# A two-layer hybrid model step on one core: prompt columns and sample tokens through the weight slabs together, or apart

## The chip, the cores and the metric

The kernel runs on one NeuronCore of a Trainium2 chip. It is one launch; the metric is its device time in microseconds. The core's engines have queues of their own: TensorE (PE, with its weight loads PEld), VectorE (DVE), ScalarE (ACT), GpSimd (POOL) and SyncE (SP, which here issues DMAs). They meet through semaphores.

## The reference, cut to what matters

512 prompt tokens and 8 x 4 = 32 sample tokens, all float32, go through the same weights. Layer 0 has a gated short convolution and an attention with forget gates over a paged cache, layer 1 a Conformer convolution module, and both a feed-forward part with a convolution on its gate branch.

```python
h = rmsnorm(x, norm_g) @ w_in                      # layer 0: 3072 columns and 8 forget gates
yp = yp + jnp.concatenate([ya, yb], axis=-1) @ w_out0[i]
a, g = jnp.split(rmsnorm(x, norm_g) @ w_pw1 + b_pw1, 2, axis=-1)     # layer 1
y, new_hist = causal_dwconv(a * jax.nn.sigmoid(g), hist, conv_w)     # width 31
return jax.nn.silu(layernorm(y + conv_b, ln_g, ln_b)) @ w_pw2, new_hist
gate, val = jnp.split(rmsnorm(x, norm_g) @ w_up, 2, axis=-1)         # both layers, 2816 each
return (jax.nn.silu(causal_dwconv(gate, hist, conv_w)[0]) * val) @ w_down
```

## The kernel before, in words

Activations lie with channels on partitions and T = 544 tokens along: columns 0 to 511 are the prompt (TP = 512), 512 to 543 the samples (TS = 32). A **slab** is one 128-column block of a weight matrix, with 8 tiles of 128x128 (6 or 5 in the down-projections, whose contraction of 2816 is cut in halves of 12 and 10 tiles; there two slabs add into one PSUM group, `per_group` = 2). Slabs go round four slots: SP loads slab s into `w_raw` (`load`), ScalarE copies it to `w_h` in the reduced-precision form fp32r (`split_high`), GpSimd subtracts for the remainder `w_l` (`split_low`). Activations are split the same way into high and low (`xa_h`, `xa_l`; `h_h`, `h_l`). TensorE's `slab` (L1768) makes three products for each tile, `w_h` with high, `w_h` with low and `w_l` with high; since a PSUM bank holds 512 numbers a partition, each runs as two matmuls of HT = 272 columns into the two banks of `pair[0]` or `pair[1]`, in turn.

`plan()` lists the phases: qkv (12 slabs), gates (12), out (8), then for each layer's feed-forward up0 (24 slabs), down0 (16, of 6 tiles), up1 (20), down1 (16, of 5 tiles), and between the two pw1 (16) and pw2 (8). The gates slabs are interleaved with the attention and have a routine of their own (`gate_half`, L2019). Others run through `gemm`, the first turn of four slabs written out, the rest in a loop.

The order on each engine is the order of the code; `turns` walks a phase with four slabs a turn, `ahead` is the preparation of the slab three further on. In an up phase the even slab j is a gate slab, the odd one a value slab. VectorE multiplies the gate slab by 1/rms (`scaled`, L1152), makes the three-tap convolution `cv`; ScalarE `sl` = silu (L1022); GpSimd `sr` = `sl` x 1/rms (L738); VectorE `tmp` = value x `sr` (L1590); ScalarE `h_h` (L1026), VectorE `h_l` (L1592). In `residual` phases VectorE adds the slab to `x` (L1529), and `norm_work` (L800, L801) squares and splits `x` for the next phase. In pw1 VectorE's `chunk` makes `u` and eleven taps of the 31-tap convolution; the others are matmuls in four column groups (`pe_conv`, L2182 and L2185), reading `u_sh`, copies of `u` that SP and ScalarE shift by DMA (`shifted`). In the attention, `value_page` (L1952) multiplies pages of cached values, likewise in four column groups, and `own_heads` (L1959) turns the result. `head_square` and `head_root` (L854, L859, L861) serve the norms of queries and keys in qkv, between slabs of which TensorE sums squares (L1864).

The semaphores that matter: `s_raw` (loaded), `s_hi`, `s_lo` (split), `s_slab` (multiplied), `s_free` or `s_xnew` (read out of PSUM).

## Time and profile before

| | us |
|---|---|
| median of 3 runs | 1512.69 (1512.01 to 1517.98) |
| the profiled execution | 1527.78 |
| its span, first to last instruction | 1525.9 |
| TensorE busy | 1440.1 |
| VectorE, GpSimd, ScalarE busy | 744.6, 587.1, 473.0 |
| mean granted clock of TensorE | 0.971 |

The rows further down are from the profiled execution. TensorE's rows show the start of each matmul and a duration that includes its passage through the array, so that consecutive ones overlap: what one costs in a row of many is the distance between starts, not the duration. An fp32 matmul leaves two records, an fp32r one a single record.

### The profile page before, as it was taken

How to read it: one execution, taken by the hardware profiler on the slowest of the kernel's cores; microseconds unless marked ns; L12 is line 12 of the kernel's file. 1: busy time of each engine (PE TensorE's matmuls, PEld its weight loads, DVE VectorE, ACT ScalarE, POOL GpSimd, SP SyncE). 2: the span in 40 equal slices, each digit the busy share in tenths (PEclk: the TensorE clock that was granted, in tenths of full speed). 3: DMA queues.
4: the chain of work that ended last, by engine and by line, in shares of the span. 5: the costliest groups of instructions: out<-in, count | busy, mean ns of one | idle time of the engine just before them, and what ended most of it. 6: DMA issues, size and time to landing. Idle time of an engine off the chain costs nothing. (4 is left out here: it accounts for less than half of the span.)

```text
span 1525.9 us, 34946 instructions
## 1 busy us (share of the span) xinstructions
PE 1440.1 (94%) x13997; PEld 1326.6 (87%) x13997; DVE 744.6 (49%) x1258; ACT 473.0 (31%) x678; POOL 587.1 (38%) x321
## 2 busy tenths in 40 slices
PE   6998898899799999999999999986999999999998
PEld 5896666666689999999999987864999999999998
DVE  5654766677443544203443369988345441044411
ACT  5374222222134222312223331116443322222221
POOL 3312222222232645445444344430435444445441
PEclk9999988999989999999999999997999999999999
DMA  5416777987732332233322446560313323323222
GB/s 177 125 52 217 244 250 256 316 281 232 237 100 69 100 93 69 84 97 96 89 70 61 131 124 158 145 159 15 109 56 92 93 70 94 107 79 91 62 78 73
DMA packets 246375, 192.56 MB, mean 126 GB/s; under 512 B 12129, under 2 KB 205106, under 8 KB 246186
## 3 DMA queue, kind: packets, MB, share of 16 engines
q1 hardware_dynamic: 244753, 188.71, 40.6%
q10 hardware_dynamic: 1373, 1.84, 0.5%
q8 instruction: 77, 1.26, 0.3%
q0 software_dynamic: 144, 0.52, 0.1%
q14 instruction: 28, 0.23, 0.0%
HBM read 173.03 MB, written 6.04 MB: 117 GB/s over the span
## 5 line engine op out<-in xcount | busy, mean ns | idle before, releaser
L664 POOL TENSOR_TENSOR w_l<-w_raw,w_h 128x1024 fp32r<-128x1024 f32 (+2 forms) x195 | 432.9, 2222 | 447.6 <-ACT w_h L791 418.8
L1768 PE MATMUL banks<-xa_h,w_h 128*128 128x272 f32 x1856 | 388.2, 290 | 4.5 <-DVE tmp L1590 3.3
L1768 PE MATMUL banks<-xa_h,w_l 128*128 128x272 f32 x1856 | 384.9, 289 | 0.0
L1768 PE MATMUL banks<-xa_l,w_h 128*128 128x272 f32 x1856 | 383.6, 288 | 0.0
L1768 PEld LDWEIGHTS banks<-xa_h,w_h 128*128 128x128 f32 x1856 | 293.3, 189 | 6.8 <-issue 5.5
L1768 PEld LDWEIGHTS banks<-xa_l,w_h 128*128 128x128 f32 x1856 | 292.6, 189 | 0.0
L1768 PEld LDWEIGHTS banks<-xa_h,w_l 128*128 128x128 f32 x1856 | 290.5, 189 | 0.0
L791 ACT ACTIVATE w_h<-w_raw 128x1024 fp32r<-128x1024 f32 (+2 forms) x193 | 185.1, 961 | 182.5 <-PE banks L1768 182.2
L1768 PE MATMUL banks<-h_h,w_h 128*128 128x272 f32 x960 | 202.4, 292 | 8.1 <-DVE h_l L1737 8.0
L1768 PE MATMUL banks<-h_h,w_l 128*128 128x272 f32 x960 | 200.7, 291 | 0.0
L1768 PE MATMUL banks<-h_l,w_h 128*128 128x272 f32 x960 | 200.2, 290 | 0.0
L1529 DVE TENSOR_TENSOR x<-banks,x 128x544 f32 (+1 forms) x48 | 34.8, 725 | 271.5 <-PE banks L1768 271.5
L1768 PEld LDWEIGHTS banks<-h_h,w_h 128*128 128x128 f32 x960 | 153.2, 191 | 10.0 <-issue 7.5
L1768 PEld LDWEIGHTS banks<-h_l,w_h 128*128 128x128 f32 x960 | 153.2, 191 | 0.0
L1768 PEld LDWEIGHTS banks<-h_h,w_l 128*128 128x128 f32 x960 | 152.0, 191 | 0.0
L738 POOL TENSOR_TENSOR sr<-sl,r_all 128x544 f32<-128x544 f32 x44 | 59.8, 1360 | 232.8 <-ACT sl L1022 232.8
L1022 ACT ACTIVATE sl<-cv 128x544 f32<-128x544 f32 x44 | 29.0, 659 | 276.8 <-DVE cv L1585 276.7
L685 POOL TENSOR_SCALAR sb<-sb,small 128x128 f32<-128x128 f32 (+3 forms) x32 | 34.7, 1083 | 180.0 <-DVE small L1336 180.0
L1152 DVE TENSOR_TENSOR gate<-banks,r_all 128x544 f32<-128x544 f32 x44 | 31.8, 724 | 110.5 <-PE banks L1768 104.7
L1590 DVE TENSOR_TENSOR tmp<-banks,sr 128x544 f32<-128x544 f32 x44 | 31.9, 725 | 107.5 <-POOL sr L738 107.5
L1262 DVE STREAM_TRANSPOSE k_grp<-k_grp 128x2048 f32<-128x2048 f32 x32 | 73.5, 2298 | 0.4 <-DMA k_grp<-in_cache_k 0.4
L1576 DVE SCALAR_TENSOR_TENSOR cv<-gate,params,cv 128x511 f32<-128x511 f32 x88 | 66.1, 751 | 12.7
(286 smaller groups left out, 1698.4 us busy)
## 6 DMA issues: line engine op xcount, KB each, us to landing
w_raw<-in_w_up SPq DMA_DIRECT2D x88, 512.0 KB, 3.6
k_grp<-in_cache_k SPq DMA_DIRECT2D x128, 256.0 KB, 4.1
v_pg<-in_cache_v SPq DMA_DIRECT2D x128, 256.0 KB, 5.2
w_raw<-in_w_in SPq DMA_DIRECT2D x24, 512.0 KB, 6.5
w_raw<-in_w_down SPq DMA_DIRECT2D x32, 384.0 KB, 3.1
w_raw<-in_w_pw SPq DMA_DIRECT2D x24, 512.0 KB, 4.1
w_raw<-in_w_down SPq DMA_DIRECT2D x32, 320.0 KB, 3.1
w_raw<-in_w_out SPq DMA_DIRECT2D x8, 512.0 KB, 6.3
```

The source lines that it names most:

```text
L664: g.tensor_tensor(w_l[:, slot, 0:n], w_raw[:, slot, 0:n], w_h[:, slot, 0:n].bitcast(F32), ALU.subtract).then_inc(s_lo, 1)
L685: g.tensor_scalar(sb[:, k % 2, 0:n], sb[:, k % 2, 0:n], rinv[:, w:w + 1], None, ALU.mult).then_inc(s_pn, 1)
L738: g.tensor_tensor(sr[:, j // 2, :], sl[:, j // 2, :], r_all[:, :], ALU.mult)\
L791: A(w_h[:, slot, 0:n], w_raw[:, slot, 0:n], ACT.Copy).then_inc(s_hi, 1)
L1022: A(sl[:, b, :], cv[:, b, :], ACT.Silu).then_inc(s_sl, 1)
L1152: V.tensor_tensor(halves(dst), gview(b), halves(r_all[:, :]), ALU.mult).then_inc(s_free, 1)
L1262: V.transpose(k_grp[slot][:, at, :].rearrange("p g x -> p (g x)"), k_grp[slot][:, at, :].rearrange("p g x -> p (g x)")).then_inc(s_tk, 1)
L1529: V.tensor_tensor(halves(flat(x[:, ds(m, 1), :])), gview(q % 2), halves(flat(x[:, ds(m, 1), :])), ALU.add).then_inc(s_xnew, 1)
L1576: V.scalar_tensor_tensor(yp, gate[:, b, 0:TP - n], w, yp, ALU.mult, ALU.add)\
L1590: V.tensor_tensor(halves(tmp[:, b, :]), gview(1), halves(sr[:, b, :]), ALU.mult).then_inc(s_free, 1)
L1768: ins = mm(out[:, half, 0:HT], w, v[:, half * HT:(half + 1) * HT], start=first and t == 0 and n == 0, stop=last and t == phase.tiles - 1 a ...
```

## The change

- The prompt's 512 columns go through each slab as one matmul per product, into one bank (`wide_bank[q][:, 0:TP]`). VectorE reads a pair's 544 columns in one piece (`gview`).
- The 32 sample tokens are computed apart (`sample_part`): for each tile, the sample activations in full fp32 (`xs_in`, `xa_s` or `h_s`, 128x32) are stationary and the raw weights `w_raw` (128x128) are moving. Tile t goes to column group t mod 4, so four partial sums of 32 tokens x 128 channels stand on the four quarters of the partitions (`by_token`, in the pair's second bank). ScalarE copies them to SBUF (`tokens_read`, into `tok_q` or `tok_f`), and one more fp32 matmul with `four_q` or `four_f` (four stacked 32x32 identities) adds the four and turns them to channels on partitions (`sample_turned`, into columns 512 to 543).
- `sample_part` stands in the middle of a slab, `sample_turned` before the last tile of a bank group. In the first bank group of a phase the part comes behind the slab, and the turn within the next slab.
- `w_raw` is read by TensorE too, so SP's next load of a slot waits for the sample part (`s_part`) instead of for GpSimd (`s_lo`).
- ScalarE copies the sample columns of activations separately in fp32 (`xa_s`, `h_s`), and high and low parts cover 512 columns. In up phases silu moves from the even to the odd turn.
- In pw1 SP issues `shifted` before the loads, two slabs earlier in the code.
- The constants, memory places, and the changed calls in qkv, pw1, pw2 and the mixers follow the same pattern and are left out here.

```diff
+    def part(self, i, j):
+
+        return i * 4 + (self.parts0 + j)
+
+    def sums(self, i, j):
+
+        return i * (4 // self.per_group) + (self.sums0 + j // self.per_group)
...
-        gview = lambda b: pair[b][:, :, 0:HT]
+        hview = lambda b: pair[b][:, :, 0:HT]
+        wide_bank = [pair[b].rearrange("p k c -> p (k c)") for b in range(2)]
+        gview = lambda b: wide_bank[b][:, 0:T]
+        by_token = lambda b: wide_bank[b][:, TP + P:TP + 2 * P]
+        tok_of = lambda phase: tok_q if phase.name == "qkv" else tok_f
...
             def load(phase, i, j, src):
                 s = phase.slab(i, j)
                 if not (isinstance(s, int) and s < SLOTS):
-                    sp.wait_ge(s_lo, s - (SLOTS - 1))
+                    sp.wait_ge(s_part, phase.part(i, j) - (SLOTS - 1))
                 sp.dma_start(w_raw[:, j, 0:phase.tiles * P].rearrange("p (k n) -> p k n", n=P), src)\
...
             for s in range(24):
                 i, j = s // 4 % 4, s % 4
+                if 6 <= s < 22 and s % 2 == 0:
+                    shifted(s // 2 - 3)
                 if s < 16:
                     load(ph["pw1"], i, j, cols(a["w_pw1"][0], i * (2 * P) + ((j % 2) * D + (j // 2) * P)))
                 else:
                     load(ph["pw2"], i, j, cols(a["w_pw2"][0], i * 512 + j * P))
-                if s >= 8 and s % 2 == 0:
-                    shifted(s // 2 - 4)
...
                 apart(m)
                 A(sq[:, b, :], x[:, ds(m, 1), :].rearrange("p a t -> p (a t)"), ACT.Square).then_inc(s_sq, 1)
-                A(xa_h[:, ds(m, 1), :].rearrange("p a t -> p (a t)"), x[:, ds(m, 1), :].rearrange("p a t -> p (a t)"),
+                A(xa_s[:, ds(m, 1), TP:T].rearrange("p a t -> p (a t)"),
+                  x[:, ds(m, 1), TP:T].rearrange("p a t -> p (a t)"), ACT.Copy, scale=par(name, m + g0)).then_inc(s_xs, 1)
+                A(xa_h[:, ds(m, 1), 0:TP].rearrange("p a t -> p (a t)"), x[:, ds(m, 1), 0:TP].rearrange("p a t -> p (a t)"),
                   ACT.Copy, scale=par(name, m + g0)).then_inc(s_xhi, 1)
+
...
+            def tokens_read(phase, i, j):
+
+                q, n = (j // phase.per_group) % 2, phase.sums(i, j)
+                act.wait_ge(s_part, phase.part(i, j) + 1)
+                if not (isinstance(n, int) and n < 2):
+                    act.wait_ge(s_turn, n - 1)
+                A(tok_of(phase)[:, q, :], by_token(q), ACT.Copy).then_inc(s_tok, 1)
...
                             b = j // 2
-                            if j % 2 == 0:
+                            tokens_read(pu, i, j)
+                            if j % 2:
                                 act.wait_ge(s_cv, k + 1)
                                 if not (isinstance(k, int) and k < 2):
                                     act.wait_ge(s_sr, k - 1)
                                 A(sl[:, b, :], cv[:, b, :], ACT.Silu).then_inc(s_sl, 1)
-                            else:
                                 act.wait_ge(s_free, pu.group(i, j) + 1)
                                 apart(i)
-                                A(h_h[:, ds(i * 2 + b, 1), :].rearrange("p a t -> p (a t)"), tmp[:, b, :],
+                                A(h_s[:, ds(i * 2 + b, 1), TP:T].rearrange("p a t -> p (a t)"), tmp[:, b, TP:T],
+                                  ACT.Copy).then_inc(s_xs, 1)
+                                A(h_h[:, ds(i * 2 + b, 1), 0:TP].rearrange("p a t -> p (a t)"), tmp[:, b, 0:TP],
                                   ACT.Copy).then_inc(s_hhi, 1)
                     turns(act, pu, turn, peel=1 if l == 0 and half == 0 else 0)
...
+            def slab_done(phase, i, j):
+
+                dve.wait_ge(s_slab, phase.slab(i, j) + 1)
+                dve.wait_ge(s_turn, phase.sums(i, j) + 1)
+
+            def scaled(dst, phase, i, j, b):
+
+                slab_done(phase, i, j)
+                V.tensor_tensor(dst, gview(b), r_all[:, :], ALU.mult).then_inc(s_free, 1)
...
-                        dve.wait_ge(s_slab, phase.slab(i, (q + 1) * phase.per_group - 1) + 1)
-                        V.tensor_tensor(halves(flat(x[:, ds(m, 1), :])), gview(q % 2), halves(flat(x[:, ds(m, 1), :])),
-                                        ALU.add).then_inc(s_xnew, 1)
+                        slab_done(phase, i, (q + 1) * phase.per_group - 1)
+                        V.tensor_tensor(flat(x[:, ds(m, 1), :]), gview(q % 2), flat(x[:, ds(m, 1), :]), ALU.add)\
+                         .then_inc(s_xnew, 1)
...
+            def sample_part(phase, i, j, moving):
+
+                q, first, last = (j // phase.per_group) % 2, j % phase.per_group == 0, j % phase.per_group == phase.per_group - 1
+                for t in range(phase.tiles):
+                    k, at = t + (0 if first else phase.tiles), 32 * (t % 4)
+                    xs = xs_in[:, k, :] if phase.name == "qkv" else moving(k)[2]
+                    ins = mm(by_token(q)[at:at + 32, :], xs, w_raw[:, j, t * P:(t + 1) * P],
+                             start=first and t < 4, stop=last and t >= phase.tiles - 4)
+                ins.then_inc(s_part, 1)
+
+            def sample_turned(phase, i, j):
+
+                q = (j // phase.per_group) % 2
+                pe.wait_ge(s_tok, phase.sums(i, j) + 1)
+                mm(wide_bank[q][:, TP:T], tok_of(phase)[:, q, :], (four_q if phase.name == "qkv" else four_f)[:, :],
+                   start=True, stop=True).then_inc(s_turn, 1)
...
-                out = pair[(j // phase.per_group) % 2]
+                out = wide_bank[(j // phase.per_group) % 2][:, 0:TP]
+                late = isinstance(i, int) and i == 0 and j < phase.per_group
                 for t in range(phase.tiles):
                     k = t + (0 if first else phase.tiles)
                     if ready:
                         ready(k)
-                    hi, lo = moving(k)
+                    if t == 2 and isinstance(i, int) and i == 0 and j == phase.per_group and phase.name != "qkv":
+                        sample_turned(phase, 0, 0)
+                    if t == phase.tiles // 2 and not late:
+                        sample_part(phase, i, j, moving)
+                    if t == phase.tiles - 1 and last and not late:
+                        if phase.name == "qkv" and i == 0 and j == 1:
+                            sample_turned(phase, 0, 0)
+                        sample_turned(phase, i, j)
+                    hi, lo, _ = moving(k)
                     wh, wl = w_h[:, j, t * P:(t + 1) * P], w_l[:, j, t * P:(t + 1) * P]
                     for n, (w, v) in enumerate(((wh, hi), (wh, lo), (wl, hi))):
-                        for half in range(2):
-                            ins = mm(out[:, half, 0:HT], w, v[:, half * HT:(half + 1) * HT],
-                                     start=first and t == 0 and n == 0,
-                                     stop=last and t == phase.tiles - 1 and n == 2)
+                        ins = mm(out, w, v[:, 0:TP], start=first and t == 0 and n == 0,
+                                 stop=last and t == phase.tiles - 1 and n == 2)
                 ins.then_inc(s_slab, 1)
+                if late:
+                    if phase.name == "qkv":
+                        pe.wait_ge(s_xs, 1)
+                    elif phase.name == "out":
+                        pe.wait_ge(s_four, 3)
+                    sample_part(phase, i, j, moving)
```

TensorE in the loop of an up phase, from the end of one slab into the next; in before each row of x2 is the two halves of 272 columns:

```order
L1768 MATMUL banks<-xa_h,w_h 128x272 x2
L1768 MATMUL banks<-xa_l,w_h 128x272 x2
L1768 MATMUL banks<-xa_h,w_l 128x272 x2
L1768 MATMUL banks<-xa_h,w_h 128x272 [waits free,lo]
L1768 MATMUL banks<-xa_h,w_h 128x272
L1768 MATMUL banks<-xa_l,w_h 128x272 x2
```

The same place now, from the middle of the slab to the next one:

```order
L1857 MATMUL banks<-xa_h,w_l 128x512
L1822 MATMUL banks<-w_raw,xa_s 32x128 x8
...
L1829 REGISTER_ALU
L1830 MATMUL banks<-four_f,tok_f 128x32 [waits sample_copied]
L1857 MATMUL banks<-xa_h,w_h 128x512
L1857 MATMUL banks<-xa_l,w_h 128x512
L1857 MATMUL banks<-xa_h,w_l 128x512
L1837 REGISTER_ALU
L1874 REGISTER_ALU [waits lo]
L1857 MATMUL banks<-xa_h,w_h 128x512 [waits free]
```

Two rows of 272 columns have become one of 512, and two blocks of another kind stand among them, the second with a wait for ScalarE.

ScalarE in the same loop before, one turn's first half (even and odd slab of the first pair):

```order
L791 ACTIVATE w_h<-w_raw 128x1024 [waits slab]
L1019 ISA
L1021 REGISTER_ALU [waits conv]
L1022 ACTIVATE sl<-cv 128x544 [waits silu_r]
L788 ISA
L790 ISA [waits raw0]
L791 ACTIVATE w_h<-w_raw 128x1024 [waits slab]
L1024 ISA
L1026 ISA [waits constants,free]
L1026 ACTIVATE h_h<-tmp 128x544
```

and now, from the odd slab's part of the turn:

```order
L821 ACTIVATE w_h<-w_raw 128x1024 [waits slab]
L839 REGISTER_ALU
L841 REGISTER_ALU [waits sample_part]
L842 ACTIVATE tok_f<-banks 128x128 [waits sample_turned]
L1068 ISA
L1070 REGISTER_ALU [waits conv]
L1071 ACTIVATE sl<-cv 128x544 [waits silu_r]
L1072 REGISTER_ALU
L1074 ISA [waits constants,free]
L1074 ACTIVATE h_s<-tmp 128x32
L1076 ISA
L1076 ACTIVATE h_h<-tmp 128x512
```

The copy of the partial sums stands between the split of the next weights and silu, and silu behind both splits.

SP in pw1 before:

```order
L414 DMA w_raw<-in_w_pw 128x8x128 [waits lo] x9
L591 DMA u_sh_140<-u 32x784 [waits conv_cleared,u]
L591 DMA u_sh_140<-u 32x784 x3
L591 DMA u_sh_140<-u 32x783 x4
L414 DMA w_raw<-in_w_pw 128x8x128 [waits lo] x2
```

and now:

```order
L441 DMA w_raw<-in_w_pw 128x8x128 [waits sample_part] x6
L621 DMA u_sh_147<-u 32x784 [waits conv_cleared,u]
L621 DMA u_sh_147<-u 32x784 x3
L621 DMA u_sh_147<-u 32x783 x4
L441 DMA w_raw<-in_w_pw 128x8x128 [waits sample_part] x2
```

Six loads instead of nine stand ahead of the first shifted copies, and the loads wait for TensorE's sample part.

## Rows read from the trace of the kernel before

**Rows 1.** The page: span, TensorE's busy time, its 40 slices, the granted clock.
```profile
span 1525.9 us, 34946 instructions
PE 1440.1 (94%) x13997; PEld 1326.6 (87%) x13997; DVE 744.6 (49%) x1258; ACT 473.0 (31%) x678; POOL 587.1 (38%) x321
PE   6998898899799999999999999986999999999998
PEclk9999988999989999999999999997999999999999
```
**Rows 2.** Busy time by stage; columns in the first row, x is the count.
```profile
core 0: us, PE busy (x) PEld busy (x) DVE busy (x) ACT busy (x) POOL busy (x), PEclk, DMA share, GB/s
500.00:600.00 100.00, 100.00 (x800) 100.00 (x800) 48.83 (x97) 27.39 (x35) 53.82 (x27) 1.00 0.30 90
136.00:138.00 2.00, 2.00 (x17) 2.00 (x16) 0.18 (x1) 0.00 (x0) 0.00 (x0) 1.00 1.06 406
332.00:341.00 9.00, 8.73 (x229) 6.33 (x227) 7.31 (x17) 3.11 (x4) 2.93 (x2) 1.00 0.79 277
389.00:393.00 4.00, 4.00 (x59) 3.64 (x58) 0.42 (x1) 0.62 (x2) 2.38 (x1) 1.00 0.06 19
...
908.00:1036.00 128.00, 114.20 (x1336) 88.82 (x1339) 115.16 (x141) 25.39 (x42) 50.63 (x21) 0.96 0.58 149
```
**Rows 3.** TensorE's waits: total us, times, longest.
```profile
PE banks L2182 <- DMA u_sh<-u: 9.6, 7, 3.6
PE banks L1768 <- DVE h_l L1737: 8.0, 4, 7.1
```
**Rows 4.** TensorE in time, up stage: start, duration, line, shapes, count.
```profile
546.80 0.41 PE L1768 MATMUL banks<-xa_h,w_h 128*128 128x272 f32 x2
...
548.81 0.41 PE L1768 MATMUL banks<-xa_h,w_l 128*128 128x272 f32 x2
```
**Rows 5.** TensorE in time: 256-column matmuls into value pages.
```profile
389.91 0.28 PE L2019 MATMUL banks<-xa_h,w_l 128*128 128x256 f32 x1
...
390.99 0.28 PE L2019 MATMUL banks<-xa_h,w_l 128*128 128x256 f32 x1
391.20 1.06 PE L1952 MATMUL banks<-v_pg,pr 128*8 128x128 f32 x32
```
**Rows 6.** TensorE in time: 288-column matmuls, then 64-row ones.
```profile
136.28 0.29 PE L2019 MATMUL banks<-xa_h,w_h 128*128 128x288 f32 x1
...
138.55 0.29 PE L2019 MATMUL banks<-xa_h,w_l 128*128 128x288 f32 x1
138.77 0.48 PE L1969 MATMUL banks<-qkv 64*128 64x256 f32 x1
```
**Rows 7.** TensorE in time: the convolution's matmuls, 32 stationary columns.
```profile
911.16 1.06 PE L2182 MATMUL banks<-u_sh,w_sh 128*32 128x512 f32 x8 [2.67 <-DMA u_sh<-u]
912.01 0.24 PE L2185 MATMUL banks<-u_sh,w_sh 128*32 128x32 f32 x5
```
**Rows 8.** TensorE in time: value pages, then a full-width transpose.
```profile
339.92 1.06 PE L1952 MATMUL banks<-v_pg,pr 128*8 128x128 f32 x32
340.91 0.33 PE L1979 MATMUL banks<-ident,sb 128*128 128x128 f32 x1
```
**Rows 9.** TensorE in time: own_heads and its neighbour.
```profile
336.25 0.40 PE L1959 MATMUL banks<-small,own 128*128 128x16 f32 x2
336.49 0.27 PE L1924 MATMUL banks<-ident,small 128*32 128x128 f32 x1
```
**Rows 10.** Line 918: ScalarE's copies out of PSUM, ns shortest/median/longest.
```profile
L918 ACT ACTIVATE pt<-banks x32: 255/426/581, 146.3 to 389.0; 128x128 f32<-128x128 f32 x8, 128x256 f32<-128x256 f32 x8, 128x384 f32<-128x384 f32 x8, 128x512 f32<-128x512 f32 x8
```
**Rows 11.** ScalarE and VectorE in time, up stage.
```profile
560.91 0.66 ACT L1022 ACTIVATE sl<-cv 128x544 f32<-128x544 f32 x1 [7.46 <-DVE cv L1585]
563.99 0.66 ACT L1026 ACTIVATE h_h<-tmp 128x544 f32 x1 [1.47 <-DVE tmp L1590]
564.56 1.04 ACT L791 ACTIVATE w_h<-w_raw 128x1024 fp32r<-128x1024 f32 x1
568.80 0.72 DVE L1152 TENSOR_TENSOR gate<-banks,r_all 128x544 f32<-128x544 f32 x1 [2.74 <-PE banks L1768]
```
**Rows 12.** TensorE and ScalarE in time, qkv stage.
```profile
75.21 1.08 PE L1864 MATMUL banks<-sq,head_ones 128*128 128x272 f32 x4
80.57 0.64 ACT L854 ACTIVATE sq<-qkv 128x544 f32<-128x544 f32 x1
81.23 1.28 ACT L859 ACT_TABLE_LOAD   x1
```
**Rows 13.** The page, DMA issues: count, size, us from issue to landing.
```profile
w_raw<-in_w_up SPq DMA_DIRECT2D x88, 512.0 KB, 3.6
w_raw<-in_w_down SPq DMA_DIRECT2D x32, 320.0 KB, 3.1
```

More of the change, by code:

```diff
@@ L106, in plan @@
         slab, groups[residual] = p.slab1, p.group1
+    part = sums = 0
+    for p in phases.values():
+        if p.name != "gates":
+            p.parts0, p.sums0 = part, sums
+            part, sums = part + p.slabs, sums + p.slabs // p.per_group
     return phases
@@ L197, in build @@
         base = top[0]
+        xa_s, _ = place("xa_s", [P, DC, T], F32, xa_at)
+        h_s, _ = place("h_s", [P, HALF[0], T], F32, hh_at)
         x_rows, _ = place("x_rows", [P, 5, D], F32, hh_at)
@@ L847, in _ @@
             A(fw_h[:, :, :], fw[:, :, :], ACT.Copy).then_inc(s_fw, 1)
+            for n in range(2):
+                tokens_read(ph["qkv"], 0, n)
             root(0)
@@ L876, in _ @@
                     head_square(n - 3)
+                if n >= 2:
+                    tokens_read(ph["qkv"], n // 4, n % 4)
                 if n == 4:
@@ L989, in _ @@
             act.wait_ge(s_sp, NGRP)
+            A(h_s[:, 4:8, TP:T], qkv[:, 0:4, TP:T], ACT.Copy).then_inc(s_xs, 1)
             for c in range(4):
-                A(h_h[:, 4 + c, :], qkv[:, c, :], ACT.Copy).then_inc(s_hhi, 1)
+                A(h_h[:, 4 + c, 0:TP], qkv[:, c, 0:TP], ACT.Copy).then_inc(s_hhi, 1)
             def residual(phase, stage, then=None, late=None):
@@ L1513, in _ @@
                 dve.wait_ge(s_hhi, 5 + c)
-                V.tensor_tensor(h_l[:, 4 + c, :], qkv[:, c, :], h_h[:, 4 + c, :].bitcast(F32), ALU.subtract)\
+                V.tensor_tensor(h_l[:, 4 + c, 0:TP], qkv[:, c, 0:TP], h_h[:, 4 + c, 0:TP].bitcast(F32), ALU.subtract)\
                  .then_inc(s_hlo, 1)
```

73 lines of the change are left out of this document (47 added, 26 removed).

## The prediction

> **What bounds the kernel now.** I read the page first, then windows by stage, then waits, then TensorE's own rows in time. TensorE is busy 1440.1 of 1525.9 us at a granted clock of 9 tenths or more in nearly every slice [rows 1]. In an up stage (500 to 600 us) it is busy without a gap, at full clock, while VectorE has 48.83, ScalarE 27.39 and GpSimd 53.82 of the 100 us [rows 2]. What it waits for there is about nothing; over the kernel the largest waits in the slabs are 9.6 us for u_sh transfers and 8.0 us for h_l [rows 3]. So outside the Conformer's first projection (pw1), whatever TensorE gains or loses in a slab is gained or lost in the end. In pw1 (908 to 1036 us) VectorE has 115.16 of 128 us and TensorE idles 13.8 [rows 2]: there VectorE sets the pace.
>
> **The old slab.** 16 matmuls of 272 columns start between 546.80 and 548.81 us, so one starts every 125.5 ns [rows 4] (800 in 100 us less the two that straddle the edge gives 125.3 [rows 2]; I use 125.3). A tile of the weights takes six, 752 ns. The work: 132 slabs of 8 tiles (qkv 12, out 8, up 88, pw1 16, pw2 8), 32 of 6 and 32 of 5 in the down phases, in all 1408 tiles, 8448 matmuls. The `gates` slabs aren't touched.
>
> **Term 1, wide prompt matmuls.** Each pair of 272 columns (250.6 ns) becomes one of 512. No fp32r matmul of 512 columns stands in the trace. Two other widths do: 256 columns start every 120 ns (389.91 to 390.99, nine steps) and 288 every 133 (136.28 to 138.55, seventeen steps) [rows 5, 6]. At 2.4 GHz, the level of full granted clock in these stretches, the columns alone are 106.7, 113.3 (for 272) and 120.0 ns, so there is an excess of 12 to 13.5 ns. If the excess is fixed per matmul, 512 columns take 213.3 + 12.7 = 226 ns; if it grows with the columns (0.461 ns each), 236. I take 230, between them. Below that end I go to the excess of the fp32 streams, which is small: two rounds of 512 fp32 columns at two cycles each take 0.85 us where the columns are 853 ns [rows 7]; then 215.8 (a rival below). At 230 a matmul saves 20.6 ns: 494 ns in a slab of 8 tiles, 742 in two slabs of 6, 618 in two of 5.
>
> **Term 2, the sample part.** A slab gets one fp32 matmul per tile: stationary 128x32 sample activations, moving 128 raw weight columns, in four column groups. The trace has nearly the same thing: the value pages (L1952), stationary 128x8, moving 128x128 fp32, four column groups. Each such matmul leaves two records. 32 records start from 339.92, the last is 0.79 us later (1.06 of the row less 0.27 of one), and the next kind starts at 340.91 [rows 8]. So eight rounds of four: seven steps and the 20 ns inside a round make 0.79, a round is 110 ns, which is the 128 columns at two cycles. Eight tiles are 16 records, four rounds: 3 x 110 + 20 = 0.35 us to the last start, plus 0.20 to the next full-width matmul. On the way in, the full-width matmul before it is followed after 0.21 instead of 0.12 (390.99 to 391.20) [rows 5], and 0.22 instead of 0.13 into a row-split kind (138.55 to 138.77) [rows 6]: +0.09. In all 0.35 + 0.20 + 0.09 = **0.64 us** a slab. Six and five tiles need the same four rounds, since tiles 4 and 5 reuse groups 0 and 1. Thirty-two stationary columns instead of eight should not matter: the convolution's matmuls have 32 and eight records of 512 columns, in two rounds, take 0.85 us [rows 7]. The lower bound is the rounds alone, 0.44.
>
> Nothing of this lies beside other TensorE work. It replaces 96 columns per tile (three passes of 32, 40 ns) by two records of 128 columns at two cycles, a quarter each, 55 ns: **the stream doesn't get shorter**, only the excess of three matmuls per tile does.
>
> **Term 3, adding and turning.** One fp32 matmul, stationary tok 128x128, moving 128x32, once per bank group: 132 + 32 = 164. Nearest is own_heads (L1959), stationary 128x128, moving 16: its two records start at 336.25, the next kind at 336.49 [rows 9], so 0.245 us, set by the weight loads, as 32 moving columns are 27 ns. Bounds: 0.055 (streams alone) and 0.245 plus a wait for ScalarE. I take **0.245**. The first bank group of each phase does its sample part behind its slab and turns within the next; the prices are the same.
>
> **What the other engines do.** ScalarE copies the 128x128 partial sums first; 128 columns out of PSUM took 255 ns [rows 10], and the turn stands before the last tile, three tiles (2.1 us) after the sample part in a slab of 8, two tiles (1.4 us) in one of 6 or 5. Queued behind the copy's wait on ScalarE are the split of the next weights, silu and h_h. In the up stage a gate slab ends at about 568.4, where VectorE's `gate` product is released (568.80), so the slabs before it end at 562.4 and 556.4; silu begins at 560.91, 4.5 us into the odd slab, h_h ends at 564.65, 2.2 us into the even one, and the next split at 565.6, 3.2 into it [rows 11]; the new copy is due at 0.64 + 4 x 0.69 = 3.4 and must be over by 5.5: covered. In qkv the cycle is tight: the head sums begin at 75.21 and take four records of 0.23, so the next slab begins at 76.1; ScalarE's square ends at 81.21 and the table load follows [rows 12]; the copy goes between them, to 81.5, against the turn at 76.1 + 5.5 = 81.6. I book 1 us for the eight slabs. A w_raw slot now comes free at the middle of its slab's matmuls instead of when GpSimd is done. SP's load then lands 3.1 us (down) or 3.6 us (up) later [rows 13], about 1.2 us into the next slab, and is first read by ScalarE's split just then, three slabs before TensorE needs it: nothing, though with 5 tiles (4.1 us a slab) the split and the copy end 2.3 us into the slab against the turn at 3.4, so 1.1 us of cover is left. The h_s and xa_s copies (0.2 us) sit in the same slack; where h_l is awaited (8.0 us [rows 3]) VectorE's chain sets it. In pw1 slabs 6.2 us longer in all hide in the 13.8 us of idleness; SP is moved to issue u_sh's transfers before the loads, and its loads' new waits (middle of slabs already run) hold up nothing.
>
> **The sum.** Slab of 8: -494 + 640 + 245 = +391 ns, times 116 = +45.4 us. Pair of 6: -742 + 1280 + 245 = +783, times 16 = +12.5. Pair of 5: -618 + 1525 = +907, times 16 = +14.5. With 1 us of qkv: **+73 us**. The profiled span goes from 1525.9 to about 1599; that execution took 1527.78 where the median is 1512.69, so the forecast is 1512.7 + 73 = **1586 us**. With 226 ns it is 1570, with 236 ns 1608.
>
> **Rivals.**
> - Wide matmuls nearly free of excess (215.8 ns). For: fp32 streams show 2 ns. Against: three fp32r widths all show 12 to 13.5. Then +50, +272 and +481 ns: +18 with qkv's 1 us, 1531 us. Chance 0.14. The Trainium skill, page "TensorE: Matmul & The Clock Gate", section "Back-to-back issue gap", gives N/2.4 + 2.5 ns for a warm matmul, which would make this the case; the fp32r rows disagree with it.
> - Faster: the array hides the changes of tiling and the turn's weight loads beneath running matmuls. Then the sample part costs 0.43, the turn 0.055, and with 226 ns a slab of 8 gains 107 ns: 1503; with 215.8 also, 1464. It decides where sample part and turn together fall under 0.59 us in a slab of 8. Against: 0.20 and 0.09 stand at every such change I read. 0.06; and 0.04 for a partial case within 0.5%. The skill's page "TensorEngine Tiling (Array Packing)", "When to Use Tiling", advises just this swap for 32 moving columns, with fourfold column tiling; its section "Key Properties" says that changing the mode drains the engine, and the 0.09 and 0.20 are that.
> - The turn waits for ScalarE, whose order puts splits or norms first. Half of 148 turns at 0.5 us: +37, 1623. For: only 0.1 and 1.1 us of cover in qkv and the 5-tile slabs. 0.08.
> - The granted clock drops because more of the time is drains: 0.9 over the 800 us of up and down stages is +80, 1666. Against: value pages and convolution ran at full clock. 0.04.
> - The change doesn't do what it says: four groups run one after another, 16 x 110 ns instead of 4 x 110 for 8 tiles: 1.3 us more in 116 slabs, 0.9 in 32 and 0.7 in 32, about +200, 1790. Against: [rows 7, 8]. 0.02.
>
> **How the numbers follow.** The forecast (226 to 236 ns, changes paid) has 0.62. The range takes in its 1570 to 1608, the first rival's 1531 and the third's 1623, and leaves out the rest, 0.16: 1528 to 1625. Faster by over 0.5% 0.06, within 0.5% 0.04, slower 0.90; 0.5% is about what a measurement of this kernel can tell from no change.
>
> **What would show it.** In an up stage: prompt matmuls starting every 226 to 236 ns; 16 sample records in 0.35 us with 0.09 more before and 0.20 after; a turn of 0.245; slabs of 6.4 us instead of 6.01; TensorE waits on tok near nothing except in qkv; pw1 no longer than before. I am wrong if the pitch is near 216 ns, if records of sample part and full-width matmuls overlap without the gap, or if waits behind tok_q or tok_f exceed a few us.

## The result, and the profile after

The changed kernel takes **1638.03 us** (median of 4 runs, 1634.55 to 1638.82) where the kernel before takes 1515.34 beside it (4 runs, 1512.01 to 1518.71): a ratio of 1.0805, 95% interval 1.0771 to 1.084. The forecast was 1586, with a range of 1528 to 1625. The direction was right; of a loss of 123 us it foresaw 73. Of parts_only, further down, one of the four executions took 2377.65 us at a granted clock of 0.558; its median is that of the other three.

The head of the page of after, to be read against [rows 1]; the first line gives span and instructions, then busy time by engine, then the slices of TensorE and its granted clock:

```profile
span 1636.7 us, 33584 instructions
...
PE 1537.9 (94%) x12917; PEld 1141.9 (70%) x12917; DVE 691.2 (42%) x1262; ACT 528.2 (32%) x923; POOL 574.0 (35%) x321
...
PE   6998889997999999999998989977989999999998
PEclk9999999998999999999999999988999999999999
```

TensorE has 1080 matmul records fewer and is busy 98 us longer, at much the same mean granted clock (0.978, before 0.971). One piece of an up stage, TensorE's rows in time (start, duration, line, result and operands, shapes, count), to be read against [rows 4]:

```profile
707.39 0.39 PE L1857 MATMUL banks<-xa_h,w_h 128*128 128x512 f32 x1
707.63 0.39 PE L1857 MATMUL banks<-xa_l,w_h 128*128 128x512 f32 x1
707.86 0.40 PE L1857 MATMUL banks<-xa_h,w_l 128*128 128x512 f32 x1
708.18 0.65 PE L1822 MATMUL banks<-w_raw,xa_s 128*32 128x128 f32 x16
708.76 0.50 PE L1857 MATMUL banks<-xa_h,w_h 128*128 128x512 f32 x1
709.09 0.39 PE L1857 MATMUL banks<-xa_l,w_h 128*128 128x512 f32 x1
709.32 0.39 PE L1857 MATMUL banks<-xa_h,w_l 128*128 128x512 f32 x1
...
710.00 0.40 PE L1857 MATMUL banks<-xa_h,w_l 128*128 128x512 f32 x1
710.24 0.30 PE L1830 MATMUL banks<-four_f,tok_f 128*128 128x32 f32 x2
710.38 0.48 PE L1857 MATMUL banks<-xa_h,w_h 128*128 128x512 f32 x1
710.70 0.39 PE L1857 MATMUL banks<-xa_l,w_h 128*128 128x512 f32 x1
```

Wide matmuls start every 0.23 us (232 ns where nothing else stands between them: wide_only's slabs of 5.573 us, below, over 24). Around the 16 sample records the starts are: last wide matmul to first record 0.32, the records 0.37 to the last start, then 0.20 to the first wide matmul (708.76), **and from that one to the next 0.33 instead of 0.23** (709.09). Around the turn: 0.24, 0.14, and again 0.32 to the second wide matmul (710.70). A slab takes 6.533 us where it took 6.013. What TensorE waits for, over the kernel and then in pw1 alone (us in total, times, longest), against [rows 3]:

```profile
PE banks L1830 <- ACT tok_f L842: 25.1, 10, 4.7
PE banks L1857 <- DVE h_l L1801: 9.2, 6, 7.1
...
PE banks L2259 <- DMA c_row<-in_state_conv_c: 5.4, 1, 5.4
...
PE banks L2277 <- DMA u_sh<-u: 3.4, 1, 3.4
```

```profile
ACT w_h L821 <- DMA w_raw<-in_w_pw: 55.1, 7, 9.6
...
PE banks L1830 <- ACT tok_f L842: 16.6, 7, 3.9
```

**By stage.** The length of a phase is read off the starts of its first and last prompt matmul in the records; "before" is a second profiled execution of the kernel before (span 1513.1 us, run beside the first experiments), "expected" is the prediction's sum laid out by phase.

| stage | before | after | difference | expected |
|---|---|---|---|---|
| qkv | 98.2 | 102.3 | +4.1 | +5.7 |
| gates and attention | 299.6 | 280.5 | -19.1 | 0 |
| out | 50.2 | 53.3 | +3.1 | +3.1 |
| four up phases | 536.0 | 587.8 | +51.8 | +34.4 |
| four down phases | 277.3 | 320.8 | +43.5 | +27.0 |
| pw1 | 132.7 | 163.3 | +30.6 | 0 |
| pw1 to pw2 | 33.4 | 35.6 | +2.2 | 0 |
| pw2 | 53.9 | 59.4 | +5.5 | +3.1 |
| sum | | | +121.8 | +73.3 |

The spans differ by 123.6, so the table holds all but 1.8 us. Three things were missed: the slabs cost more, pw1 grew by 30 us where nothing was expected, and the attention became 19 us shorter.

### The profile page after: what moved, and what is told of

Read it like the earlier page. It is cut to its first block, busy times and chain, and to the rows that moved or that the text cites. A ratio compares the mean times of both kernels' runs of the same rounds, so it can differ in the third digit from the quotient of the medians.

```text
span 1636.7 us, 33584 instructions
## 1 busy us (share of the span) xinstructions
PE 1537.9 (94%) x12917; PEld 1141.9 (70%) x12917; DVE 691.2 (42%) x1262; ACT 528.2 (32%) x923; POOL 574.0 (35%) x321
## 4 chain that ended last, share of the span: by engine, by line
PE 80%; issue 5%; DVE 5%; DMA 4%; ACT 3%; SPq 2%; POOL 1%; ACTq 1%; DVEq 0%; POOLq 0%
PE banks L1857 58%; PE banks L1822 6%; PE banks L2114 4%; SPq L621 2%; PE banks L1993 1%; PE banks L1830 1%; PE banks L2047 1%; DMA w_raw<-in_w_pw 1%; DMA v_pg<-in_cache_v 1%; PE banks L2087 1%; PE banks L2064 1%; DVE k_grp L1325 1%; PE banks L2001 1%; ACTq L1118 1%; POOL w_l L694 1%
## 5 line engine op out<-in xcount | busy, mean ns | idle before, releaser
L1857 PE MATMUL banks<-xa_h,w_h 128*128 128x512 f32 x928 | 391.8, 422 | 0.8 <-POOL w_l L694 0.4
L1857 PE MATMUL banks<-xa_h,w_l 128*128 128x512 f32 x928 | 368.4, 397 | 0.0
L1857 PE MATMUL banks<-xa_l,w_h 128*128 128x512 f32 x928 | 368.1, 397 | 0.0
L1857 PEld LDWEIGHTS banks<-xa_h,w_h 128*128 128x128 f32 x928 | 176.9, 191 | 54.2 <-issue 23.6
L1857 PE MATMUL banks<-h_h,w_h 128*128 128x512 f32 x480 | 204.3, 426 | 9.3 <-DVE h_l L1801 9.2
L1857 PEld LDWEIGHTS banks<-xa_h,w_l 128*128 128x128 f32 x928 | 176.3, 190 | 39.4
L1857 PEld LDWEIGHTS banks<-xa_l,w_h 128*128 128x128 f32 x928 | 177.0, 191 | 30.7
L1857 PE MATMUL banks<-h_l,w_h 128*128 128x512 f32 x480 | 190.7, 397 | 0.0
L1857 PE MATMUL banks<-h_h,w_l 128*128 128x512 f32 x480 | 190.6, 397 | 0.0
L1857 PEld LDWEIGHTS banks<-h_h,w_h 128*128 128x128 f32 x480 | 91.3, 190 | 44.9 <-issue 23.6
```

Source lines behind the costliest of these rows:

```text
L1857: ins = mm(out, w, v[:, 0:TP], start=first and t == 0 and n == 0, stop=last and t == phase.tiles - 1 and n == 2)
```

## The experiments

### The three terms one by one

The question: are the three terms of a slab what the sum has, or does the rest of the loss come from somewhere else? Three kernels take parts of the change away, a fourth is the kernel before itself.

wide_only (no sample matmuls, no turns):

```diff
-                    if t == phase.tiles // 2 and not late:
-                        sample_part(phase, i, j, moving)
...
-                dve.wait_ge(s_turn, phase.sums(i, j) + 1)
+                dve.wait_ge(s_part, phase.part(i, j) + 1)
...
             def sample_turned(phase, i, j):
+                return
```

(A prompt matmul in the middle of the slab signals `s_part`.)

> Leaves out the sample matmuls, ScalarE's copies of the partial sums and the turning matmuls; the sample columns are not computed. The semaphore of the sample part is raised by a prompt matmul at the same place. Both theories below have the same value here: 4224 matmuls of 512 columns every 231 ns (measured in the changed kernel) for 8448 of 272 every 125.3, so -83 us: about 1432 against 1515 of before. If the pitch is not what the up stage shows, or other waits come up, it is off by more than 10 us.

parts_only adds the sample part again, turns_only the copies and turns instead:

> The sample matmuls are there, the copies and the turning matmuls left out, so the sample columns are not computed. Theory A (leaving the column groups costs 0.31 us and not 0.20, since the first full-width matmul afterwards takes 0.1 longer; a part is 0.77): 196 x 0.77 = +151 us over wide_only, about 1583. Theory B (a part costs the 0.64 of the prediction and the excess is waits for ScalarE and SP): +125, about 1557.

> The sample matmuls are left out, the copies of the partial sums and the turning matmuls are there, so the sample columns are wrong. Theory A: 164 turns of 0.22 = 36 us, and the waits for ScalarE's copy at three phase starts (12 us) and in pw1 (some 13 us): +61 over wide_only, about 1493. Theory B: 40 us and more waits, +77 or more.

> The kernel before once more, for its profile: the attention stage from the end of qkv to the first out slab took 306.8 us in the first profile and 280.5 in the changed kernel's. If that difference is chance, this profile has a stage well under 300 and a span near 1512; if the change made it, 306 again.

| kernel | median us | ratio to before (95%) | slab of 8, us |
|---|---|---|---|
| wide_only | 1480.89 | 0.9761 (0.971 to 0.9812) | 5.573 |
| turns_only | 1532.24 | 1.0118 (1.0058 to 1.0177) | 5.773 |
| parts_only | 1599.49 | 1.0546 (1.0475 to 1.0616) | 6.33 |
| changed kernel | 1638.03 | 1.0805 (1.0771 to 1.084) | 6.533 |

Slab by slab the three terms are clean: the wide matmuls gain **0.440 us** (0.494 booked), the turn costs **0.200** (0.245 booked), the sample part **0.757** (0.640 booked). Together +0.52, as in after. In the totals part and turn come to 119 and 51 us over wide_only, where their theories A had 151 and 61. Phase by phase against wide_only, the part's shortfall lies in pw1 (9 us of its 12 don't show), qkv (6), up00 and up10 (3 each) and an attention stage 5.5 us shorter; in down00 and up01 it is paid in full. And the wide matmuls brought only 35 us, not the 83 expected, where the slabs alone gain 132 x 0.44 + 32 x 0.34 + 32 x 0.28 = 78 us. Something took more than half of it; that is the question of the third group of experiments. before_again took 1514.96 us, its attention stage 299.6, where the first profile of the same kernel had 306.8.

### What the sample part consists of

The sample part of slabs of 8 is done twice: in one kernel in direct succession, in the other (the diff) at a quarter and at half of the slab. In the first the tiling is entered and left once, in the second twice.

```diff
+                    if t == phase.tiles // 4 and phase.tiles == DC and not late:
+                        sample_part(phase, i, j, moving, False)
                     if t == phase.tiles // 2 and not late:
                         sample_part(phase, i, j, moving)
```

> The changed kernel with each sample part in the middle of a slab of 8 tiles issued twice in direct succession (124 of them; the second starts its sums anew). Theory A (a part is 0.37 us of rounds plus 0.40 of going in and out of the column groups): four more rounds, 0.39 each, +48 us, some less in pw1: about 1682. Theory B (the prediction's prices, rounds 0.44, changes 0.29): +55, about 1692. The kernel after this one decides between them.

> The same number of sample matmuls as in the kernel before this, but the first set two tiles earlier, so that the column groups are entered and left twice. Theory A: 0.40 us more each than together, so +48 us over it, about 1730. Theory B: 0.29 - 0.09 for what rounds hide, 0.20 to 0.29 each, +25 to +36, at most 1720. If changes of tiling cost nothing, the same as together.

1698.14 us together (ratio 1.1178, 1.1131 to 1.1225), 1737.23 apart (1.1432, 1.1386 to 1.1479). TensorE's rows in time, first of the kernel with both together, then of the other:

```profile
756.34 0.40 PE L1860 MATMUL banks<-xa_h,w_l 128*128 128x512 f32 x1
756.66 1.08 PE L1822 MATMUL banks<-w_raw,xa_s 128*32 128x128 f32 x32
757.68 0.50 PE L1860 MATMUL banks<-xa_h,w_h 128*128 128x512 f32 x1
758.01 0.40 PE L1860 MATMUL banks<-xa_l,w_h 128*128 128x512 f32 x1
```

```profile
765.62 0.65 PE L1822 MATMUL banks<-w_raw,xa_s 128*32 128x128 f32 x16
766.19 0.50 PE L1860 MATMUL banks<-xa_h,w_h 128*128 128x512 f32 x1
766.53 0.39 PE L1860 MATMUL banks<-xa_l,w_h 128*128 128x512 f32 x1
...
767.78 0.64 PE L1822 MATMUL banks<-w_raw,xa_s 128*32 128x128 f32 x16
```

Sixteen more records in succession make the slab 6.973 us, 0.440 more than 6.533: four rounds of 110 ns. Apart it is 7.307, another **0.334 us for one more way in and out**. So 0.44 of a part is streaming and 0.33 is the change of tiling, for which the sum had 0.20 (its 0.64 less four rounds); a single part, 0.757, leaves 0.32. The totals agree in kind: 60 us more together (theory B's price of rounds had 55), another 39 apart, between B's 36 and A's 48. The stream alone, 0.440, already eats the 0.440 that the wide matmuls gain in a slab of 8, and more than they gain in the shorter ones: by these prices this way of treating the samples can't win in the slabs even with the change of tiling and the turn at nothing.

### Where the wide matmuls' gain went, and pw1's 30 us

The suspicion: SP's new order and waits hold up pw1. In wide_only, ScalarE's splits wait 69.0 us for `w_raw` loads in pw1; the 16 `u_sh` transfers stand in SP's queue ahead of every second load. Against it stands the prediction's reading, that VectorE sets pw1's pace. The kernel before with the new order (the diff), and the changed kernel with one load ahead of the transfers:

```diff
                 i, j = s // 4 % 4, s % 4
+                if 6 <= s < 22 and s % 2 == 0:
+                    shifted(s // 2 - 3)
...
-                if s >= 8 and s % 2 == 0:
-                    shifted(s // 2 - 4)
```

> The kernel before with only SP's order in pw1 as the change has it: the shifted copies two slabs earlier, ahead of the loads, which wait for GpSimd as before. Theory S: TensorE does not wait for a turn here, so at most the splits are later; within 5 us of before. Rival (the early copies themselves slow pw1 down, as pw1 is 10 us longer in wide_only although its matmuls are shorter): +10 us or more, 1525.

> The changed kernel, in pw1 with SP's next even load issued ahead of the 16 shifted copies instead of behind them (but for the last). Theory S (in pw1 ScalarE's split waits for a load that stands behind 9.6 us of issues, the copy of the partial sums stands behind that split, and TensorE's turn behind the copy): 13 of the 16.6 us of waits in pw1 go, about 1623. Rival (the waits come from ScalarE's own DMA issues and the square root at the phase's start): at most -3 us, 1635.

The first: 1537.71 us, ratio 1.014 (1.0093 to 1.0187); pw1 146.8 instead of 132.7, the gap behind it 40.8 instead of 33.4. **The order alone costs the kernel before some 20 us**, and the higher of the two expectations was still too low. The second: 1646.99 us (1.0845, 1.0794 to 1.0895), pw1 165.4: both expectations missed. In its pw1 the waits for tok fell from 16.6 to 7.4 us, and waits for `u_sh` of 13.6 came in their place: the wait moved. With two loads ahead, the nearest to the order before:

> Nothing is left out. Against the changed kernel (1638.0 us) only SyncE's order in pw1 changes: two loads, then the 16 u_sh transfers of a block, the closest to the order before that the new load waits allow. Theory (ScalarE's split_high waits for loads that stand behind u_sh transfers): with both loads ahead, w_h's waits for w_raw fall from 55 us to under 25, pw1 falls from 163 to 145 to 152 us and the total to 1620 to 1627. Rival (with one load ahead the wait had only moved to u_sh; with two it moves there again): pw1 160 or more, PE's waits for u_sh 10 us or more, total 1635 to 1650.

1704.9 us (1.1261, 1.1225 to 1.1297), 67 more than the changed kernel, and pw1 takes 210.5. The waits in its pw1:

```profile
PE banks L2279 <- DMA u_sh<-u: 51.9, 6, 10.0
...
ACT w_h L823 <- DMA w_raw<-in_w_pw: 21.5, 6, 3.8
```

The split's waits fell as expected, and the rest went wrong: the load of slab 2c+7 now waits until TensorE has done the sample part in the middle of slab 2c+3, right behind which the convolution needs block c of `u_sh`, whose 16 transfers stand behind that load and take 10 us to issue. No order of one queue serves both: what ties them is that a load waits for TensorE. Two kernels remove that tie. One is wide_only with before's waits and order:

```diff
-                    sp.wait_ge(s_part, phase.part(i, j) - (SLOTS - 1))
+                    sp.wait_ge(s_lo, s - (SLOTS - 1))
```

> Work left out: the sample tokens' products and the turns, so their columns of the output are wrong; all else is computed. Against the wide-matmul kernel (1480.9 us) only SyncE changes: its loads wait for GpSimd's split again (s_lo), and the u_sh transfers stand behind the loads as in the kernel before. The wide slabs themselves gain 0.44 us x 132 slabs (and 0.33 x 32, 0.28 x 32), about 75 us, of which only 35 arrived; pw1 had grown by 10 us and the wait for c_row took 5.5. Theory (SyncE's new order and waits ate part of the gain): pw1 128 to 134 us, no c_row wait, total 1455 to 1468. Rival (VectorE and ScalarE set the pace of pw1, and the order does not matter): within 4 us of 1480.9.

The other keeps all matmuls, but moves the high halves through the sample part, so that nothing but the splits reads `w_raw`, and it has before's waits and order too:

```diff
-                    ins = mm(by_token(q)[at:at + 32, :], xs, w_raw[:, j, t * P:(t + 1) * P],
+                    w = w_h[:, j, t * P:(t + 1) * P].bitcast(F32)
+                    ins = mm(by_token(q)[at:at + 32, :], xs, w,
...
-                    sp.wait_ge(s_part, phase.part(i, j) - (SLOTS - 1))
+                    sp.wait_ge(s_lo, s - (SLOTS - 1))
```

> What is changed in the computation: the sample products take the high halves of the weights (w_h) as moving operand instead of the raw weights, so the samples' outputs are less exact; number, shape and type of all matmuls stay. With that, nobody but the splits reads w_raw, so SyncE's loads wait for GpSimd's split as in the kernel before, and the u_sh transfers stand behind the loads as there. Theory S (TensorE's reading of the raw weights binds SyncE's loads to TensorE, which costs pw1 some 20 us, pw1 to pw2 a few and the c_row wait 5): slabs still 6.533 us, pw1 140 to 146 us instead of 163, no c_row wait, total 1605 to 1612. Rival R (the tok copies behind the splits and the root, and VectorE, set pw1's length whatever SyncE does): pw1 158 or more, total 1628 to 1638.

wide_loads_as_before takes **1454.83 us**, ratio 0.9621 (0.9584 to 0.9657): 26 less than wide_only by nothing but SP's waits and order. pw1 fell from 144.3 to 127.9 us, down01 from 72.0 to 62.5 (c_row's wait of 5.5 is gone), the gap behind pw1 from 43.6 to 32.9. With slabs of 5.573 us as in wide_only, 60 of the 78 us now arrive. Of the other 18, qkv holds the most: its twelve slabs gain 5.3 and it takes 98.4 us, as before; what holds it was not tried. high_half_moving takes 1619.09 us (1.0681, 1.0646 to 1.0716), 19 less than the changed kernel; pw1 is 148.1, the gap 33.2. It is nearer to S than to R, though S had 140 to 146 for pw1 and a total under 1612. Waits and order went back together here, so how the 19 us divide between them is not shown. The waits in its pw1, where the splits no longer wait for a load, and a window over it (us, then busy time of PE, PEld, DVE, ACT, POOL with instructions, the clock, DMA share and GB/s):

```profile
ACT w_h L818 <- PE banks L1855: 19.0, 7, 2.9
...
PE banks L1828 <- ACT tok_f L839: 7.4, 2, 4.2
```

```profile
913.00:1061.00 148.00, 139.78 (x1300) 94.14 (x1299) 82.36 (x144) 34.81 (x61) 57.19 (x24) 0.98 0.52 136
```

What is left of pw1's growth, 148.1 less 132.7, is sixteen slabs at 0.52 (8.3) and the waits for tok (7.4). TensorE is busy 140 of 148 us, and VectorE 82.

### The waits at the starts of phases

ScalarE's first copy of partial sums stands behind `root()`, which waits for VectorE's sums; `c_row`'s load stands behind all of down01's loads, which now wait for TensorE.

```diff
             def ffn(l):
+                tokens_read(ph[f"up{l}0"], 0, 0)
                 root(SQ["out" if l == 0 else "pw2"])
```

(The same ahead of pw1's root; the copy in the turn is left out, and `c_row` is loaded after down01's first turn.)

> Nothing is left out. Against the changed kernel (1638.0 us): at the start of up00, up10 and pw1 ScalarE copies the first partial sums ahead of the root, and SyncE issues the c_row load after the first turn of down01's loads. Theory: the three starts lose 3.3 + 4.7 + about 3.5 us of TensorE's wait on tok_f, and c_row's 5.4 goes: total 1638 - 16 = 1622 (1619 to 1626). Rival (the root was late because VectorE's sums are late, so TensorE waits for the same VectorE chain a little later): total within 5 us of 1638.

> Nothing is left out. Both edits in one: two loads ahead of the u_sh transfers, and the early copy and c_row. If they are independent the gains add: 1638 - 16 - (the gain of the order alone); by the theory 1604 to 1612, by its rival 1622 to 1636. In either case it stays above the kernel before (1515), since the up-stage slabs alone cost 60 us more: this is the bound on what the new waits contribute.

> As the kernel before this one in the call (samples from the high halves of the weights), and in addition ScalarE copies the first partial sums of up00, up10 and pw1 ahead of the root. If both causes are right and apart, the total is that kernel's less 8 us, 1597 to 1604, and what is left over the kernel before is the slabs alone: 116 x 0.52 + 16 x 1.07 + 16 x 1.15 + 16 x 0.52 = 104 us less what pw1 hides. If the waits were one and the same, no gain over the other kernel.

copy_and_c_row_early takes 1626.63 us (1.0749, 1.0712 to 1.0786), 11.4 less, where 16 was expected: down01 is 6.6 us shorter, so c_row's part is as expected, and up00, up10 and pw1 together only 6.5, little more than half of what their waits had shown. The waits moved on by a turn. In up00 3.3 us at the first turn became 2.4 at the next, in up10 4.7 became 2.4, and in pw1 3.2 and 3.9 became one of 6.2, so that the sum over the kernel fell only from 25.1 to 22.2:

```profile
PE banks L1837 <- ACT tok_f L845: 22.2, 10, 6.2
```

The other kernels of this group: all_three, with the order of two_loads_before_shift, takes 1689.47 (1.1149, 1.1108 to 1.119), 15 less than that kernel, with pw1 still at 211.5. high_half_and_copy_early takes 1610.74 (1.0632, 1.0598 to 1.0666), 8.4 less than high_half_moving: the two causes are apart, and 94 us over the kernel before beside it (1516.33) are left.

### Splitting the samples off as a matmul of their own

The kernel before with 512 + 32 columns instead of 272 + 272, all in fp32r, with nothing in column groups:

```diff
-                        for half in range(2):
-                            ins = mm(out[:, half, 0:HT], w, v[:, half * HT:(half + 1) * HT],
+                        for a0, a1 in ((0, TP), (TP, T)):
+                            ins = mm(out[:, a0:a1], w, v[:, a0:a1],
```

> Nothing is left out. The kernel before, but each pair of matmuls of 272 columns is one of 512 prompt columns and one of 32 sample columns (same stationary weights, same fp32r passes), results in one span of 544 columns over two banks. Before, a pair takes 251 ns; the 512 columns alone measured 231. Theory A (the excess over the columns grows with them, 0.46 ns each): 32 columns cost 15 to 27 ns, the pair 246 to 258, total 1500 to 1535. Theory B (each matmul has its own weight load, as many LDWEIGHTS as MATMULs in the profile, and a load of 128 columns does not fit under 32): the pair 285 ns or more, slab 6.85 us or more, total 1635 or more. Under B the sample columns can't simply be split off, and 272 + 272 is the better cut.

**2034.93 us**, ratio 1.3418 (1.3365 to 1.3471), 400 us above the least that theory B had. Two stretches of it, TensorE in an up stage (a row holds the matmul of 512 and that of 32) and in out, then windows over both (out first):

```profile
700.13 0.50 PE L1772 MATMUL banks<-xa_h,w_h 128*128 128x512 f32 x2
700.48 0.49 PE L1772 MATMUL banks<-xa_l,w_h 128*128 128x512 f32 x2
```

```profile
499.61 0.80 PE L1772 MATMUL banks<-h_l,w_h 128*128 128x512 f32 x2
500.25 0.80 PE L1772 MATMUL banks<-h_h,w_l 128*128 128x512 f32 x2
```

```profile
445.00:568.00 123.00, 123.00 (x386) 104.33 (x385) 18.75 (x27) 18.60 (x26) 18.98 (x8) 0.50 0.14 41
610.00:770.00 160.00, 160.00 (x931) 139.32 (x930) 45.95 (x101) 31.03 (x39) 59.68 (x30) 1.00 0.21 61
```

At full clock a pair takes 344 ns (a slab 8.267 us), where 272 + 272 take 251 and 512 alone 231. The 32 columns thus cost 113 ns, though their stream is 13. That is the side of theory B, but double its 55 ns; as each matmul has a weight load of its own, and the load behind the 32 columns is as long as any other (PEld 139 of 160 us; the two loads of a pair start 108 ns apart, at 700.108 and 700.216), the loads fit, but that they are the cause was not tested. All eight slabs of out and of pw2 ran at a granted clock of 0.50 on top (1.2 GHz), 15.36 us each: 113 of the 519 us, the longer pairs being nearly all the rest (93 ns times 4224 is 393).

## Why the prediction was wrong, point by point

- **Wide matmuls: right in kind, 2 ns short.** 232 ns, from ends of 226 and 236 and a choice of 230; over 4224 matmuls the 2 ns are 9 us (0.440 for 0.494 in a slab). The Trainium skill, page "TensorE: Matmul & The Clock Gate", section "Back-to-back issue gap", gives N/2.4 + 2.5 ns for an isolated warm matmul, an estimate of 215.8 for 512 columns, and about 131 ns for 512 columns in a sustained stream. The trace agrees with neither: at 256, 272, 288 and 512 columns it has 13.3, 12, 13.5 and 19 ns over the columns. The excess grows somewhat with the columns, less than in proportion.
- **The sample part: right in its mechanism, too small in one term.** The rounds of 110 ns, the 0.09 in and the 0.20 out were all there. The step that failed is "plus 0.20 to the next full-width matmul": I stopped counting at the *start* of the first matmul behind the change, and that one then holds its successor up by another 0.10 us (708.76 to 709.09). 0.757 in place of 0.640. The Trainium skill, page "TensorEngine Tiling (Array Packing)", section "Key Properties", says that a change of mode drains the engine; the runs fit that and give the price, 0.334 us in and out.
- **The turn**: 0.200 for 0.245.
- A slab of 8 came to +0.52 in place of +0.391, a pair of 6 to 80.5 less 72.0 over eight pairs, +1.06 (booked 0.783), a pair of 5 to 75.7 less 66.5 over eight, +1.15 (booked 0.907). In all about +95 us of slabs where 73 were booked: 22 of the 50 missed.
- **"In pw1 slabs 6.2 us longer in all hide in the 13.8 us of idleness"**: wrong, and with it the first part, that VectorE sets the pace there. The window that I read, 908 to 1036 us [rows 2], is not pw1, whose slabs run from 883.4 to 1017.5. Cut at 1017, it has 5.9 us of TensorE's idleness inside pw1 and 7.9 in the 19 us behind it. In the second execution of the same kernel TensorE is busy 129 of 132 us of pw1, and VectorE 90 where the first had 115 of 133. The windows, two of the first execution and one of the second:

```profile
908.00:1017.00 109.00, 103.13 (x1200) 84.17 (x1200) 99.69 (x117) 21.11 (x34) 49.88 (x21) 1.00 0.59 149
1017.00:1036.00 19.00, 11.08 (x138) 4.65 (x141) 15.47 (x25) 4.28 (x8) 0.74 (x1) 0.73 0.54 149
```

```profile
876.00:1008.00 132.00, 128.88 (x1392) 108.94 (x1391) 89.68 (x144) 30.22 (x44) 61.01 (x25) 0.99 0.59 152
```

  The same taps took 1.06 us each in the first execution and 0.72 in others (the two lines below, of before and of high_half_moving), and pw1 was no more than 1.4 us longer for it. A stage that does not follow a change of 25 us in an engine's work isn't bound by that engine. TensorE was the bound, with a few us of waits: wide_loads_as_before shortened pw1 by 4.8 us (its slabs alone by 7.0), high_half_moving lengthened it by 15.4 (its slabs alone by 8.3, and the waits for tok by 7.4).

```profile
L1670 DVE SCALAR_TENSOR_TENSOR tmp<-u,params,tmp 128x488 f32<-128x488 f32 (+4 forms) x34 | 36.1, 1062 | 0.0
```

```profile
L1731 DVE SCALAR_TENSOR_TENSOR tmp<-u,params,tmp 128x490 f32<-128x490 f32 (+4 forms) x35 | 25.0, 716 | 0.0
```

- **"Its loads' new waits (middle of slabs already run) hold up nothing"**: wrong; of the failed steps outside the slabs it is the dearest. SP is a queue too: 10 us of issuing `u_sh` ahead of every second load make the loads late, and loads that wait for TensorE tie the transfers that TensorE needs to its own progress. Price: 19 us in the changed kernel (high_half_moving), 26 with wide matmuls only, 20 as the order alone in the kernel before. The first two include c_row's wait of 5.4 behind down01's loads, which the prediction's walk along SP's queue did not reach.
- **The copy under cover**: right inside the phases but pw1 (outside it TensorE waits for tok_f in 3 of 136 turns), and qkv even came out at +4.1 where 5.7 was booked; wrong in pw1, where 7 of 16 turns wait, and at the starts of up00 and up10, where `root()` stands ahead of the copy. I had worked the cover out in a turn of the loop and not in the first. 25.1 us of waits, of which 16.6 in pw1.
- **The attention's 19 us** were not foreseen. They are a gain that hides part of the error: without them the sum would have missed by 69 us.
- The rivals: of the free wide matmuls, the hidden change of tiling, the dropped clock (0.978; its price was +89 by its own figures, not +80) and the serial groups none came. The third, "the turn waits for ScalarE", named the right wait at the wrong place; at 1623 it was also the nearest.

No version here beats the kernel before with the whole result computed. wide_loads_as_before shows the room: 60 us, if 32 tokens could be had for less than 0.44 us a slab. The two ways tried cost 0.96 and 2.7.

## What to carry to other kernels

Price a change of the array's tiling by the distance from the last matmul before it to the *second* one behind it, and ask whether the new work's bare stream is already as long as what it replaces. When a buffer gets a new reader, follow the wait into the queue that refills it and list all that stands behind in that queue, to the end of the phase. And don't call an engine the bound by its busy share in one execution: cut the window at the stage's own first and last matmul, look at a second execution, or at whether the stage followed when that share changed.

## What was not expected of the hardware

- **The attention stage** lasts 276 to 283 us in seven kernels that have sample parts and turns as in after, 294 to 307 in before (two profiles) and in the kernels without sample parts, 289 with parts alone, and 297 to 300 with doubled parts. Its matmuls are the same in all. Waits of the value pages without a releaser that the profile shows are 9.7 us in before (the first line) and not among the stage's eleven largest waits in after, the least of which is 1.2, and the granted clock over the stage is 0.93 and 0.97 (windows of before and of after):

```profile
PE banks L1952 <- issue: 9.7, 6, 2.7
```

```profile
117.00:418.00 301.00, 264.91 (x4375) 199.30 (x4373) 191.94 (x353) 83.83 (x161) 78.67 (x56) 0.93 0.79 260
```

```profile
123.00:404.00 281.00, 251.00 (x4364) 189.84 (x4363) 191.32 (x353) 81.76 (x164) 78.58 (x56) 0.97 0.82 275
```

  The waits go with the length: TensorE's idle time ahead of value-page matmuls adds up to 9 to 15 us in each of the nine profiles of 294 us or more, and to about 3 in each of the eight of 289 or less. The clock does not: wide_only has 0.96 in a stage of 294.1 us, copy_and_c_row_early 0.95 in one of 283.0. What the waits are for, and what in the kernel moves them, stays open.
- **A clock that stays down.** In wide_and_32 the granted clock was 0.85 in the last 20 us of the attention, where TensorE was busy 11.5 of 20 us, and then 0.50 for all 123 us of out, in which TensorE's rows show no gap. It was still 0.50 in the first slabs of up00, up to 588 us, and 0.97 in the 20 us behind that. In the changed kernel the last 23 us of the attention have 0.85 as well, and out then runs at 0.92 in its first 20 us and at 1.00 in the next. It was seen in pw2 again, so it is no accident of one stretch. The mix of matmuls alone doesn't do it, since the same mix runs at 1.00 in the up stages; what keeps the clock down was not tried.
- **VectorE's taps** took 1.06 us in one execution and 0.72 in the next of the same kernel, and pw1, where they run, was only 1.4 us longer for it.
